# First-layer expert weights in 4 MB transfers with 32 KB runs per partition, second-layer ones in 2 MB

## The reference

```
logits = (xf @ router_w + router_b)                      # 288 tokens x 32 experts
top_val, top_idx = lax.top_k(logits, TOP_K)              # TOP_K = 4
gates = jax.nn.softmax(top_val, axis=-1)
...
def expert_block(args):                                  # for each of the 32 experts
    xb, e = args
    hid = xb @ moe_w1[e] + moe_b1[e]                     # (1024 x 2048): 8.4 MB
    gate = jnp.minimum(hid[:, :D_FF], SWIGLU_LIMIT)
    lin = jnp.clip(hid[:, D_FF:], -SWIGLU_LIMIT, SWIGLU_LIMIT)
    act = gate * jax.nn.sigmoid(SWIGLU_ALPHA * gate) * (lin + 1.0)
    return act @ moe_w2[e] + moe_b2[e]                   # (1024 x 1024): 4.2 MB
```

## Time and profile before

| | |
|---|---|
| median of 3 runs | 1119.19 us (1118.88 to 1120.93) |
| the profiled execution: its time | 1119.61 us |
| its span, first to last instruction | 1117.9 us |
| PE busy | 1078.0 us, 96% of the span |
| DVE, ACT, POOL busy | 31%, 14%, 4% |
| moved by DMA | 425.63 MB, 381 GB/s over the span |
| transfers of expert weights | 192 of 2048 KB |
| mean granted clock of TensorE | 0.986 of 2.4 GHz |

### The profile page before, as it was taken

One profiled execution on the slowest core, in us unless ns is written; L12 is line 12 of the kernel. 1 busy time (PEld: TensorE's weight loads), 2 busy tenths in 40 slices (PEclk: granted clock), 3 DMA queues, 4 the chain that ended last, 5 costly groups with the idle time before them and its releaser, 6 DMA issues.

```text
span 1117.9 us, 13864 instructions
## 1 busy us (share of the span) xinstructions
PE 1078.0 (96%) x5441; PEld 472.0 (42%) x5441; DVE 349.6 (31%) x829; ACT 160.1 (14%) x307; POOL 40.9 (4%) x101
## 2 busy tenths in 40 slices
PE   7999999999999999999999999999999999999996
PEld 4677547343434343434343333333333343434342
DVE  4797663313131313131313131212121213122124
ACT  4254604000100010001000100010101010101002
POOL 8000400000000000000000000000000000000000
PEclk9999997999999999999999999999999999999998
DMA  9533645999999999999999999999999999999992
GB/s 294 193 151 158 265 193 214 401 427 428 427 429 429 427 429 429 427 429 429 427 430 429 428 429 429 428 429 429 427 429 430 427 429 430 427 430 429 429 427 82
DMA packets 41094, 425.63 MB, mean 381 GB/s; under 512 B 6073, under 2 KB 12606, under 8 KB 16489
## 3 DMA queue, kind: packets, MB, share of 16 engines
q1 hardware_dynamic: 39185, 423.61, 90.5%
q0 software_dynamic: 1888, 1.75, 0.6%
HBM read 423.38 MB, written 2.17 MB: 381 GB/s over the span
## 4 chain that ended last, share of the span: by engine, by line
PE 73%; DMA 23%; DVE 2%; ACT 1%; issue 0%; SPq 0%; DVEq 0%
PE bank L1785 33%; DMA ring<-in_moe_w_dram 23%; PE bank L1800 10%; PE bank L1441 9%; PE bank L1742 7%; PE bank L1755 5%; PE bank L1698 2%; PE bank L1468 1%; PE bank L1810 1%; PE bank L1750 1%; PE bank L1446 1%; PE bank L1664 0%; PE bank L1688 0%; PE bank L1842 0%; DMA xt<-in_x_prompt_dram 0%; PE bank L1580 0%
## 5 line engine op out<-in xcount | busy, mean ns | idle before, releaser
L1785 PE MATMUL bank<-ring,hT 128*64 128x512 f32 x2048 | 454.9, 595 | 17.0 <-DMA ring<-in_moe_w_dram 16.8
L1785 PEld LDWEIGHTS bank<-ring,hT 128*64 128x64 f32 x2048 | 141.6, 137 | 302.3 <-issue 275.3
L1800 PE MATMUL bank<-ring 128*64 128x512 f32 x1024 | 226.8, 595 | 0.0
L1800 PEld LDWEIGHTS bank<-ring 128*64 128x64 f32 x1024 | 70.7, 137 | 132.6 <-issue 126.0
L1339 DVE TENSOR_SCALAR ring<-bank 128x512 f32<-128x512 f32 x32 | 22.1, 692 | 322.2 <-PE bank L1785 322.2
L1742 PEld LDWEIGHTS bank<-ring 128*128 128x128 f32 x792 | 93.3, 196 | 26.3 <-issue 26.0
L1742 PE MATMUL bank<-ring 128*128 128x128 f32 x792 | 99.7, 284 | 0.2 <-DVE ring L1286 0.2
L1356 DVE COPY ring<-bank 64x512 f32<-64x512 f32 x32 | 22.2, 694 | 230.1 <-PE bank L1800 230.1
L875 ACT ACTIVATE ring<-ring 128x512 f32<-128x512 f32 x32 | 20.1, 630 | 395.0 <-DVE ring L1339 395.0
L1292 DVE COPY hT<-bank 128x512 f32<-128x512 f32 x33 | 22.7, 688 | 140.3 <-PE bank L1742 140.3
L1755 PE MATMUL bank<-ring 128*128 128x512 f32 x128 | 63.5, 618 | 0.0
(11 more groups left out here) (300 smaller groups left out, 609.1 us busy)
## 6 DMA issues: line engine op xcount, KB each, us to landing
ring<-in_moe_w_dram SPq DMA_DIRECT2D x192, 2048.0 KB, 30.5
ring<-in_w_in_dram SPq DMA_DIRECT2D x5, 1536.0 KB, 13.3
ring<-in_w_out_dram SPq DMA_DIRECT2D x2, 2048.0 KB, 11.2
ring<-in_w_in_dram SPq DMA_DIRECT2D x1, 2048.0 KB, 13.3
lnbc<-in_ln_g_dram SPq DMA_DIRECT2D x3, 512.0 KB, 11.6
lnbc<-in_ln_b_dram SPq DMA_DIRECT2D x3, 512.0 KB, 11.4
xt<-in_x_prompt_dram SPq DMA_DIRECT2D x2, 512.0 KB, 3.9
ring<-in_state_gla_dram POOLq DMA_DIRECT2D x4, 144.0 KB, 5.3
```

The source lines that it names most:

```text
L1785: ins = pe.matmul(bank[b][64 * h:64 * h + 64, :], xT[:, q, k, j * CAP:(j + 1) * CAP], ring[:, c:c + 512], start=False, stop=k == KT - 1)
L1800: ins = pe.matmul(bank[OUT_BANK[j]][64 * h:64 * h + 64, :], actT[:, j, k % 4, (k // 4) * CAP:(k // 4 + 1) * CAP], ring[:, c:c + 512], star ...
```

## The change

`w1_half` and its two transfers per first-layer block become `w1_piece` and one transfer of 4 MB, 128 runs of 32 KB, into both slots, in `load_first` and in `load_group`. It is issued when both slots are free (`room(k + 1)`), and it signals `w_full` alone. PE's wait for `w_half` in `first_layer` is gone, so PE waits for all 4 MB ahead of k = 0 and k = 4. The second layer keeps its transfers of 2 MB and both its semaphores; since `w_half` is now used by the second layer alone, once per group and semaphore, PE waits for 16 * (gi + 1) there. The order of the pieces, the ring, and all arithmetic stay.

```diff
-        def w1_half(e, s, h):
-            return moe_w1[0, bass.ds(e, 1), s * 4 * P:(s + 1) * 4 * P, :].rearrange("a (p t) c -> p (a t c)", t=4)[
-                :, h * SLOT:(h + 1) * SLOT]
+        def w1_piece(e, s):
+            return moe_w1[0, bass.ds(e, 1), s * 4 * P:(s + 1) * 4 * P, :].rearrange("a (p t) c -> p (a t c)", t=4)
...
             def load_first(f):
                 e, c = divmod(f, 2)
-                for h, signal in ((0, w_full[f]), (1, w_half[f])):
-                    sp.dma_start(slots(2 * f + h, 1), moe_w1[0, e, c * 4 * P:(c + 1) * 4 * P, :].rearrange(
-                        "(p t) c -> p (t c)", t=4)[:, h * SLOT:(h + 1) * SLOT]).then_inc(signal, 16)
+                sp.dma_start(slots(2 * f, 2), moe_w1[0, e, c * 4 * P:(c + 1) * 4 * P, :].rearrange("(p t) c -> p (t c)", t=4)
+                             ).then_inc(w_full[f], 16)
...
                             if k < first:
                                 continue
-                            ei = expert(2 * q + j)
-                            src = [w1_half(ei, c, h) for h in range(2)]
-                            room(k)
-                            sp.dma_start(slots(k % SLOTS, 1), src[0]).then_inc(w_full[k // 2 % 4], 16)
+                            src = w1_piece(expert(2 * q + j), c)
                             room(k + 1)
-                            sp.dma_start(slots(k % SLOTS + 1, 1), src[1]).then_inc(w_half[k // 2 % 4], 16)
+                            sp.dma_start(slots(k % SLOTS, 2), src).then_inc(w_full[k // 2 % 4], 16)
...
                                 if k % 4 == 0:
                                     pe.wait_ge(w_full[f % 4], 16 * (gi * 3 + f // 4 + 1))
-                                if k % 4 == 2:
-                                    pe.wait_ge(w_half[f % 4], 16 * (gi * 3 + f // 4 + 1))
...
                                 if k == 4:
-                                    pe.wait_ge(w_half[f % 4], 16 * (gi * 3 + f // 4 + 1))
+                                    pe.wait_ge(w_half[f % 4], 16 * (gi + 1))
```

## The result

The changed kernel takes 1121.33 us, median of 20 runs (1118.17 to 1124.42), the kernel before 1118.99 us in 20 runs beside it (1115.43 to 1121.41). The ratio is 1.002, 95% interval 1.0011 to 1.0029: slower by 0.2%, +2.3 us by the medians.

A forecast was written before the change was run, and what follows sets the result against it. The prediction took the DMA queue of expert weights as the bound. From 1119.6 us, 4.2 gained by rate, 3.5 lost to work left behind and 2.5 to the refill gave 1121.4 (1121.0 on the median); range 1117.5 to 1125.0.

The forecast's parts named there:

- What bounds the kernel: Expert loop: the DMA queue at 428.4 GB/s, needing 58.7 us a pair against PE's 56.8, sets the end.
- 1. The rate, 4.2 us gained: First-layer weight transfers: a 32 KB run saves 9.2 ns against two of 16 KB, over 57 transfers 4.2 us.
- the two bounds: Limits on the gain from longer first-layer runs: nothing at the lower, 8.3 us at the upper.
- 2. Work left behind, 3.5 us lost: Last pair: k = 0 waits for the whole 4 MB, so 16 records more follow the decisive landing, 3.5 us.
- 3. The refill, 2.5 us lost: Ring refill at pair 1: first transfer issued later, DMA dry longer; 2.5 us, between 1.9 and at most 3.4.
- The sum: Whole kernel: 1119.6 - 4.2 + 3.5 + 2.5 = 1121.4 us, or 1121.0 on the scale of the median, +0.16%.
- The run isn't the unit: Rival, first-layer transfers: 32 KB is cut in two or cost isn't per run, no gain; 1124.5 to 1125.2 us, chance 0.16.
- long runs shed more: Rival, first-layer transfers: rate near 434.9 GB/s, gain 8.3 us, 1116.9 us on the median; chance 0.08.
- A second dry spell at 233: Rival, stream near 233 us: the 0.9 us margin goes, losing 1.4 to 2 us; 1122.4 to 1123, chance 0.12.
- The clock falls: Rival, last pair: one 2.3 us PE gap drops the clock to 1.2 GHz, costing 1.6 us; 1122.6, chance 0.14.
- within 0.2%: Whole kernel: the forecast case, 1119.0 to 1121.4 us, too near the time before to tell apart; chance 0.50.
- The signs: Profile after: 64 transfers of 4096 KB, 128 of 2048; 301.4 MB; one 2.3 us wait, 75.4 us to the end.

The follow-up runs named there:

- twin with 16 KB runs: The changed kernel, with each 4 MB transfer made of two 16 KB runs per partition lying apart in HBM; 1.0060 of the time of the kernel before.
- 8 KB kernel: The kernel before, with each 2 MB first-layer transfer made of two 8 KB runs per partition lying apart in HBM; 1.0069 of the time before.
- halves issued late: The kernel before, with both 2 MB halves of a first-layer block issued only when both slots are free; median 1123.36 against 1118.68 us, ratio 1.0050.

## Why the prediction was right, step by step

- **What bounds the kernel**: right. Three edits that touch only the stream or what follows its last landing moved the time by what they take there. One reading was wrong: the 39 waits of 39.0 us are not waits of the matmuls alone. Theirs were 15 of 16.8 us in all, the other 24 were weight loads. Nothing in the sum rested on it.
- **1. The rate, 4.2 us gained**: right, 4.7 by the landings and 4.3 by the rates of the twin with 16 KB runs. The cost per run, drawn from 4 and 16 KB, held beyond both sizes. Of the two bounds neither came near. By the 3 cycles per packet of the Trainium skill, DMA: Bandwidth & Descriptors, "Why small descriptors are slow (HBM only)", the term would have been 1.6 us, an estimate that the runs don't bear out.
- **2. Work left behind, 3.5 us lost**: 3.4 measured, alone and together with the rest.
- **3. The refill, 2.5 us lost**: the mechanism was right, the term was sized too low. It measured 3.4 alone and 3.3 in the twin, the upper bound. The windows say where the 0.9 us are. In 208 to 220 us both versions moved 2.8 us' worth less than before (120 and 429 GB/s, 137 and 410, for 328 and 418), 0.3 more than the term. In 220 to 240, where I had said that the transfers hold, they lost another 0.8 and 0.5 us (404 and 411 GB/s for 421). In the changed kernel itself the same stretches, 3 us earlier, show 2.4 and 0.3 us (287 for 373 GB/s, 414 for 421).
- **The sum**: +1.8 forecast, -4.7 + 3.4 + 3.3 = +2.0 measured. The errors of terms 1 and 3, 0.5 and 0.9 us, partly cancelled, so it is in part luck that the sum came within 0.2 us. Nor is it a test that the measured terms add up, since the landing of the twin stands in two of them; with 4.3 us by the rates they make +2.4, and two landings of the same stream differ by 0.4.
- **The rivals.** *The run isn't the unit* and *long runs shed more* are both excluded, by the twin and the 8 KB kernel. *A second dry spell at 233*: a little of it, far from the 1.4 to 2 us of the rival; 410 GB/s in 223 to 237, where before stands at 421 in 220 to 240, is worth some 0.4 us, and up to 0.8 with halves issued late. *The clock falls*: the mechanism exists, which one row of before had suggested, and in the pairs before the last it goes into the slack, as said. In the last pair no profile shows it, but only the changed kernel's had a gap of over 2 us there. If it followed there as often as elsewhere, 15 times in 40, it would be a likelier rival than its 0.14 and cost 0.6 us on the mean, an estimate; how often it happens there in the runs, whose times spread over 6 us in both kernels, stays open. The warning of the Trainium skill, TensorE: Matmul & The Clock Gate, "Why this matters for your kernels", starts at gaps of about 3 us. Gaps of 2.0 to 2.6 us were enough here.
- The chance for "within 0.2%" and the place of the median, at +0.2%, agree only just; the time itself was 0.3 us off.
- **The signs**: there are 64 transfers of 2048 KB and not the 128 that I wrote, a slip in counting (192 less 128 halves) that nothing rested on; 301.50 MB for 301.4, one wait of 2.13 us for 2.3, and 75.3 us to the end for 75.4 came as forecast.

## What to carry to other kernels

Where one queue of transfers is the bound from start to end, ask of an edit three things apart: what it does to the rate, to the gaps while the queue is still empty, and to the work that remains behind the last landing. Larger transfers cost in the second and third, and longer runs gain in the first; the pieces between can be large while those at both ends stay small, and that version beat both kernels here. Fewer waits of an engine that waits for the bound are no gain, and a count of waits is to be read by engine before it is used.

## What was not expected of the hardware

- A PE gap of 2.0 to 2.6 us amid dense matmuls was followed 15 times in 40 by a stretch at 1.2 GHz that cost some 1.7 us (24 records in 7.07 for 5.37 us), while two gaps of some 1.15 us with 3.6 us of matmuls between them never were, in 23 pairs.
- The cost of a run is the same some 9 ns (8 to 10) from 4 to 32 KB, though at 32 KB it is under 1% of the run.
- The same mixer put the start of the loop at 183.5 us in one profile and at 186.1 to 187.1 in nine, which is more than the whole effect of the change: single spans could not be compared, stretches could.
